# Two more projections per pair of heads, and one more MLP slab per layer, computed with seven quarter products

## The reference

```python
def mixer_a(h, w_qkv, q_gain, k_gain, w_o, cos, sin):
    qkv = (h @ w_qkv).reshape(B, S, A_GROUPS, 3, A_HEADS, HEAD_DIM)
    for g in range(A_GROUPS):
        q = partial_rope(rms_norm(qkv[:, :, g, 0], q_gain[g]), cos, sin)
        k = partial_rope(rms_norm(qkv[:, :, g, 1], k_gain[g]), cos, sin)
        v = qkv[:, :, g, 2]
        num, den, mx = dilated_group(q, k, v, dil, radius)
...
    return o @ w_o

def mlp_sq_relu(h, w1, w2):
    return jnp.square(jax.nn.relu(h @ w1)) @ w2
```

## Time and profile before

| | |
|---|---|
| three runs | 2148.38 us median (2146.53 to 2149.68) |
| profiled execution, own time | 2145.56 us |
| its span, first to last instruction | 2143.8 us |
| busy: PE, PEld, DVE, ACT | 2038.7, 1305.9, 917.8, 309.6 us |
| mean granted TensorE clock | 0.988 of full |
| HBM read | 622.86 MB |

### The profile page before, as it was taken

The page is one execution under the profiler, slowest core; times in us unless marked ns, Lnnn a source line. Parts: engine busy times, 40 slices in busy tenths (PEclk is TensorE's granted clock), DMA queues, the critical chain, the costliest instruction groups (busy, mean ns, idle before and its releaser), DMA issues.

```text
span 2143.8 us, 25203 instructions
## 1 busy us (share of the span) xinstructions
PE 2038.7 (95%) x10414; PEld 1305.9 (61%) x10414; DVE 917.8 (43%) x1862; ACT 309.6 (14%) x651; POOL 0.2 (0%) x4
## 2 busy tenths in 40 slices
PE   9999999999999999999999999888999999988888
PEld 5676778999888999866734333333657644333333
DVE  4555654777222688445443222222256422222212
ACT  1232331000100000123301000000224101000000
POOL 0000000000000000000000000000000000000000
PEclk9999999999999999999999999999999999999999
DMA  8333345689444589442689999999944699999997
GB/s 326 118 121 142 141 158 200 245 318 347 157 150 179 220 314 329 161 158 98 266 344 405 428 426 427 428 427 427 386 147 171 240 401 405 428 426 428 428 427 323
DMA packets 117868, 625.46 MB, mean 292 GB/s; under 512 B 5760, under 2 KB 8448, under 8 KB 85632
## 3 DMA queue, kind: packets, MB, share of 16 engines
q1 hardware_dynamic: 116752, 619.06, 72.8%
q10 hardware_dynamic: 1008, 4.87, 0.6%
HBM read 622.86 MB, written 1.05 MB: 291 GB/s over the span
## 4 chain that ended last, share of the span: by engine, by line
PE 78%; DMA 17%; DVE 3%; ACT 1%; issue 1%; SPq 0%; DVEq 0%; ACTq 0%
PE ps L2796 14%; PE ps L2191 10%; PE ps L2258 8%; PE ps L2154 8%; PE ps L2217 7%; PE ps L2834 7%; DMA ring<-in_w_up 5%; PE ps L2464 4%; DMA spare<-in_w_down 4%; DMA spare<-in_w_gate 4%; DMA spare<-in_w_up 4%; PE ps L2272 3%; PE ps L2457 3%; PE ps L2636 2%; PE ps L2346 1%; PE ps L2771 1%
## 5 line engine op out<-in xcount | busy, mean ns | idle before, releaser
L2796 PE MATMUL ps<-ring,work_rows 128*64 128x512 f32 x1248 | 452.0, 615 | 27.6 <-DMA ring<-in_w_up 12.5
L2796 PE MATMUL ps<-arena,work_rows 128*64 128x512 f32 x584 | 261.5, 600 | 21.3 <-DMA ring<-in_w_up 9.7
L2796 PEld LDWEIGHTS ps<-ring,work_rows 128*64 128x64 f32 x1248 | 141.1, 141 | 229.2 <-issue 226.0
L2834 PE MATMUL ps<-ring,arena 128*64 128x512 f32 x608 | 215.5, 609 | 11.9 <-DMA ring<-in_w_down 6.7
L2191 PE MATMUL ps<-arena,ring 128*128 128x256 f32 x1024 | 224.7, 379 | 0.0
L2191 PEld LDWEIGHTS ps<-arena,ring 128*128 128x128 f32 x1024 | 192.7, 189 | 27.4
L2258 PE MATMUL ps<-ring,work_rows 128*128 128x384 f32 x544 | 181.9, 488 | 1.6 <-DMA ring<-in_a_wqkv 1.2
L2154 PE MATMUL ps<-work_rows,ring 128*128 128x256 f32 x640 | 140.4, 380 | 3.6 <-ACT work_rows L850 2.4
L2258 PEld LDWEIGHTS ps<-ring,work_rows 128*128 128x128 f32 x544 | 100.7, 190 | 67.1 <-DMA ring<-in_a_wqkv 1.9
L2834 PE MATMUL ps<-arena 128*64 128x512 f32 x288 | 128.4, 599 | 7.5 <-DMA ring<-in_w_down 6.8
L2796 PEld LDWEIGHTS ps<-arena,work_rows 128*64 128x64 f32 x584 | 78.1, 137 | 93.7 <-issue 88.9
(11 more groups left out here) (397 smaller groups left out, 2381.4 us busy)
## 6 DMA issues: line engine op xcount, KB each, us to landing
ring<-in_mlp_w SPq DMA_DIRECT2D x32, 2048.0 KB, 13.1
ring<-in_w_up SPq DMA_DIRECT2D x32, 2048.0 KB, 35.1
ring<-in_w_gate SPq DMA_DIRECT2D x28, 2048.0 KB, 34.3
arena<-in_w_mod SPq DMA_DIRECT2D x24, 2048.0 KB, 8.1
ring<-in_w_down SPq DMA_DIRECT2D x24, 2048.0 KB, 35.5
arena<-in_w_gate SPq DMA_DIRECT2D x20, 2048.0 KB, 26.2
ring<-in_a_wqkv SPq DMA_DIRECT2D x24, 1536.0 KB, 6.8
arena<-in_w_down SPq DMA_DIRECT2D x18, 2048.0 KB, 27.7
```

The lines of the kernel that those rows point to most:

```text
L2796: e = te.matmul(bank(b)[SB * h:SB * h + SB], xs(k, col, SB), slabs.chunk(m + h, k), start=(k == 0), stop=(k == KD - 1), skip_group_check=True)
L2834: e = te.matmul(bank(6 + o)[SB * h:SB * h + SB], ueT[a][:, P * k + SB * h:P * k + SB * h + SB], slabs.tile(m + h).rearrange("p (k n) -> p ...
```

## The change

The k and q projections of pairs 1 to 7 use the seven products too (`project_seven` replaces `project_v`), so 21 projections (`BY_SEVEN = 3 * (KD - 1)`) are done so, and not 7. Slab 1 of `w1` in each MLP layer becomes `hidden_by_seven(-1, ...)`, so 14 slabs, and not 12.

What comes with it:

- VectorE makes the weight sums of all three slabs of a pair: those of q before `join_v` of the pair before, those of k and v after it. With q and k, `gain_q` is replaced by `join_qk` (three additions of 192 columns into `raw_a`, and one multiplication by the gain over 768 columns) and `sum_qk` (the two reductions); `root_q` moves behind `scale_prob`.
- ScalarE copies four partial sums for each of q and k (`part`), copies one quarter out (`last_qk`), and squares from SBUF (`square_raw`), each at a new place in its queue.
- TensorE waits for the weight sums before the first product of each projection, and for the join of the projection before it ahead of the second.
- In the MLP, `token_sums` and `weight_sums` of slab 1 come ahead of `token_mean`; `spread` is placed after the first of the seven products, with a wait for ScalarE's copy of it before the fourth; `rotary_angles` moves behind the loop (the buffers `seven` are shifted so as not to touch the positions).

The diff's core: `join_qk` and `sum_qk`, VectorE's loop over the pairs, TensorE's loop over the pairs, and TensorE's part of the MLP.

```diff
-BY_SEVEN = KD - 1
+BY_SEVEN = 3 * (KD - 1)
...
+            def join_qk(c, w):
+                ring.wait_done(dve, A_QKV + 3 * c + w)
+                dve.wait_ge(s_copied, 4 * nth(c, w) + 4)
+                for n, cols, at in ((0, slice(0, HALF_A), 256), (1, slice(HALF_A, WIDTH_A), 0)):
+                    own.inc(ve.tensor_tensor(raw_a[w][:, 0, cols], bank(1)[:, at:at + HALF_A], part_a[w][n], ALU.add))
+                own.step(ve.tensor_tensor(raw_a[w][:, 1, HALF_A:], part_a[w][2], part_a[w][3], ALU.add))
+                dve.sem_inc(s_joined, 1)
+                dve.wait_ge(unit_read, 6 * c + 2 * w + 2)
+                ve.tensor_tensor(qk_n[:, w], raw_a[w], gain_a[:, w].unsqueeze(1).broadcast_to([P, NT, WIDTH_A]), ALU.mult
+                                 ).then_inc(q_gained, 2)
+            def sum_qk(c, w):
+                for r in range(NT):
+                    dve.wait_ge(k_squared, 4 * (c - 1) + 2 * w + r + 1)
+                    ve.tensor_reduce(ss_a[:, w, r], sq_a[r].rearrange("p (h d) -> p h d", h=6), AX, ALU.add
+                                     ).then_inc(q_summed, 1)
...
             for c in range(KD + 1):
                 for w in range(2):
-                    if c < KD:
+                    by_seven = 0 < c < KD
+                    if by_seven:
+                        join_qk(c, w)
+                    elif c < KD:
                         gain_q(c, 2 * w)
                         gain_q(c, 2 * w + 1)
...
-                    if c < KD:
+                    if by_seven:
+                        sum_qk(c, w)
+                    elif c < KD:
                         root_q(c, w)
                     if c > 0:
                         scale_prob(c - 1, 2 * w)
                         scale_prob(c - 1, 2 * w + 1)
+                    if by_seven:
+                        root_q(c, w)
                     if c < KD:
                         norm_q(c, w)
-                if 0 < c < KD:
-                    join_v(c)
                 if c == 0:
                     row_sums()
                 if c + 1 < KD:
-                    weight_sums(c + 1)
+                    weight_sums(c + 1, 0)
+                if 0 < c < KD:
+                    join_v(c)
+                if c + 1 < KD:
+                    weight_sums(c + 1, 1)
+                    weight_sums(c + 1, 2)
...
             for c in range(KD):
-                project(c, 0)
                 if before:
+                    project_seven(c, 0)
                     turn_q(c - 1, 3)
+                    project_seven(c, 1)
+                    scores(c - 1, 0)
...
+                    project_seven(c, 2)
                     turn_p(c - 1, 0)
                     turn_p(c - 1, 1)
+                    project_seven(c, 3)
                     values(c - 1, 0)
                     scores(c - 1, 1)
...
             hidden(0, n, fresh=2 * l + 1)
             sums(2 * l + 1, 6)
-            hidden(1, n + 1)
-            spread(2 * l + 1, 6)
+            hidden_by_seven(-1, n + 1, 0)
             down(0, n + 2, start=True)
```

More of the change, by code:

```diff
@@ L451, in program @@
         spare[:, 3072:3584], spare[:, 3584:4096], tmp_b[:, 0:512], tmp_b[:, 512:1024])]
-    seven = [positions[:, S * n:S * n + S].rearrange("p (k t) -> p k t", k=2) for n in range(4)]
+    seven = [positions[:, S + NT + S * n:S + NT + S * n + S].rearrange("p (k t) -> p k t", k=2) for n in range(4)]
     take = carve2()
@@ L957, in _ @@
                 now, before = c < KD, c > 0
-                if now:
+                if now and before:
+                    part(c, 0, 0, 1, 0)
+                    part(c, 0, 2, 2, 1)
+                    part(c, 0, 1, 3, 0)
+                    copy_q(c - 1, 3)
+                    part(c, 0, 3, 4, 0)
+                    last_qk(c, 0)
+                    square_raw(c, 0, 0)
+                    square_raw(c, 0, 1)
+                elif now:
                     square_q(c, 0)
-                if before:
+                    square_q(c, 1)
+                else:
                     copy_q(c - 1, 3)
-                if now:
-                    square_q(c, 1)
-                if before:
+                if now and before:
+                    part(c, 1, 0, 1, 0)
+                    prob(c - 1, 0)
+                    part(c, 1, 2, 2, 1)
+                    prob(c - 1, 1)
+                    part(c, 1, 1, 3, 0)
+                    copy_p(c - 1, 0)
+                    copy_p(c - 1, 1)
+                    part(c, 1, 3, 4, 0)
+                    last_qk(c, 1)
+                    square_raw(c, 1, 0)
+                    copy_o(c - 1, 0)
+                    copy_q(c, 0)
+                    square_raw(c, 1, 1)
+                    part(c, 2, 0, 1, 0)
+                    prob(c - 1, 2)
+                    part(c, 2, 2, 2, 1)
+                    prob(c - 1, 3)
+                    part(c, 2, 1, 3, 0)
+                elif before:
                     prob(c - 1, 0)
                     prob(c - 1, 1)
-                if now:
-                    square_q(c, 2)
-                if before:
                     copy_p(c - 1, 0)
                     copy_p(c - 1, 1)
-                if now:
-                    square_q(c, 3)
-                if before:
                     copy_o(c - 1, 0)
[L976 to L983, removed]
                     prob(c - 1, 2)
```

154 lines of the change are left out of this document (92 added, 62 removed).

## The result

The changed kernel runs in 2136.28 us (median of 4 runs, 2135.98 to 2139.64), the kernel before in 2149.03 (median of 4). The ratio is 0.9945, 95% interval 0.9927 to 0.9962: faster by 8 to 16 us. The forecast was 2136, range 2128 to 2142. The profiled execution is the slowest of the four: own time 2139.64, span 2137.8; the other three have spans of 2134.2 to 2134.7. It began late: pair 0's last plain projection starts at 46.12, where it started at 42.55 before. So I compare stages of the trace and not ends.

A forecast was written before the change was run, and what follows sets the result against it. TensorE was taken to bound the kernel, waiting for nothing in the attention stage. Savings of 17.8 (attention) and 2.8 (MLP), less waits of 1.6 and 6.6, gave −12.4 us: 2136 against the median 2148.4, 8-in-10 range 2128 to 2142.

The forecast's parts named there:

- What bounds the stage: Attention stage: TensorE busy for all 37.67 us of a pair, waiting for nothing; afterwards one idle gap per pair.
- What seven products save: Attention q and k projections: 9.20 us each instead of 10.41 and 10.53, saving 2.54 per pair, 17.8 over seven pairs.
- the rival about banks and waits: Attention q and k share banks and waits with attention work, so half the saving is lost: −2.1 us, 2146; chance 0.03.
- The loads of the short products: Seven-product projections: weight loads stay hidden; unhidden, an estimated 2.6 us per projection would mean a loss of some 18 us.
- The wait per pair: Start of pairs 2 to 7: TensorE waits 1.1 us for VectorE's chain from last exponential to q's weight sums; 6.6 in all.
- Pair 1: Start of pair 1: VectorE's row sums and q sums end at 49.54, TensorE ready at 48.04; wait 1.6 us with signal.
- Attention in sum: Attention stage: 17.8 us saved on q and k, less waits of 1.6 and 6.6, a gain of 9.6 us.
- The MLP: Slab 1 of both MLP layers: 13.89 us becomes 12.51, saving 1.38 each, 2.8 us together.
- the rest of the MLP edits: MLP token sums, weight sums, spread and moved rotary tables: cost nothing; spread at most 0.5 us per layer.
- The clock was a rival: New attention gaps let TensorE's clock fall; one pair at half speed costs about 35 us, 2171; chance 0.01.
- The sum: Whole kernel: −17.8 + 1.6 + 6.6 − 2.8 = −12.4 us, forecast 2136 against the median 2148.4.

The follow-up runs named there:

- the same addition ahead (paid) and behind (free): Changed kernel plus a 0.95 us VectorE addition, ahead of next q's weight sums: attention stage 7.6 us longer; behind v's weight sums: 295.57 against 295.62.
- −10.9 in the second: Changed kernel unedited, run again beside its two parts, against the kernel before: 10.9 us faster by the medians.

## Why the prediction was right, and where it was off

- *What bounds the stage.* TensorE without a wait before, one gap per pair after: as forecast.
- *What seven products save.* q was forecast at 9.20 and took 9.28, k 9.32. The transposes of the probabilities next to k gave 0.15 back (0.87 for 1.02), so a pair without its wait is 2.51 shorter, where 2.54 was forecast (37.67 against 36.26 − 1.10). The rows of v carried over to q and k; the share that the rival about banks and waits put in doubt is there. The loads of the short products stayed hidden, as the rows of before had said.
- *The wait per pair.* Forecast 1.1, from a chain summed step by step to 15.4 after the end of k against TensorE's 14.3; measured 15.39, and 1.10 by starts. That it is a chain and not VectorE's load was shown by the same addition ahead (paid) and behind (free).
- *Pair 1.* Forecast 1.6; the gap reads 1.50, and by starts it is 53.27 − 51.28 − 0.33 = 1.66.
- *Attention in sum.* Forecast 9.6, measured 9.3.
- *The MLP.* Forecast 2.8, measured 1.1: this is the term that was mis-sized. 13.89 to 12.51, 1.38 of gain, was right for one MLP (1.34). In the other the clock fell to the lower level over the first of the short products and took back 1.6. What failed inside this term is that I costed the rest of the MLP edits at nothing, with 0.5 per layer as the upper end. The clock was a rival only for the attention gaps, by the argument that the gap of 1.21 in the earlier trace rows had left it at 1.00. The gap is the same, but what follows it is now short products and not plain ones. The gap's length alone is not the cause, since gaps of 1.2 and 1.5 in the attention stage had no fall. With a matmul in the gap neither MLP had a fall, in one traced execution; that it is the short products behind the gap that let it fall, and not something else that changed there, was not separated. The kernel with only the attention part has the gap, plain products and no fall in either MLP.
- *The sum.* Forecast −12.4; the traces' stages give −9.3 − 1.1 = −10.4 (0.3 of the 2.0 missing is attention's, 1.7 the MLP's); the medians give −12.8 in the first set of runs and −10.9 in the second. The forecast's 2136 next to 2136.28 is therefore partly luck: the 2 us that were not gained are covered by the spread between executions.
- *The wait's cure.* The prediction priced the chain but did not ask which of its links had to be in it. The root of k did not: ahead of the scaling it costs 0.47 per pair and saves the whole wait. The root of q is better where the change put it: ahead of the scaling too, it makes A 11.1 longer (302.94 against 291.83).

## What to carry to other kernels

When work moves from a saturated engine to one that is half idle, sum the chain of that engine's queue up to the next point where the saturated one wants something; its total load says little (an addition of 0.95 us was free in one place and cost 0.99 in another, at the same load). Before adding an operation to an in-order queue, list what each neighbour is waited for, since the order that suits one half of a loop (q) need not suit the other (k). And a wait belongs in front of the first instruction that reads the value, but look at what stands behind it: the next wait may be on the same chain.

## What the runs showed of the hardware

TensorE's granted clock fell to its lower level behind short gaps, and not each time: in the MLP behind a gap of 1.16 that follows eight instructions of one column, in 12 of 22 places, where short products follow; in the attention stage never behind 0.93, 1.2 or 1.5, once in six behind 1.92, and three times in six behind 2.92. A fall cost 1.6 to 1.7 us. One matmul of 416 columns in the gap of 1.16 went with no fall in both MLPs of the one execution that was traced.

At the very start the same clock is part of why executions of one kernel differ by several us. The 48 instructions of pair 0 took 15.7 us at the full clock (16.2 in the kernel before, which waits 0.4 among them), 17.3 to 17.4 with a fall behind 32 instructions of one column, and 18.8 in one trace where the fall lasted longer. The falls came in just those executions in which the first weights had kept TensorE waiting longest (2.29 to 3.58 against 1.24 to 1.72), with the kernel's start unchanged. That the wait causes the fall was not tested.
